# Banded attention's front: keys first, then queries, two score units, and the value tiles after them

## The reference, cut to what matters

```python
qkv = h @ w_qkv + b_qkv                       # 512 x 1536: 1024 query, 256 key, 256 value columns
q = qkv[..., :Hq * Dh]
k = qkv[..., Hq * Dh:(Hq + Hk) * Dh]
v = qkv[..., (Hq + Hk) * Dh:]
...                                           # each block of 128 queries sees its own and the previous 128 keys
s = jnp.einsum('bnqkgd,bnjkd->bnkgqj', qb, kb) * (Dh ** -0.5)
s = s - slopes * dist; s = jnp.where(mask, s, -inf)
m = jnp.maximum(s.max(axis=-1), sink)
p = jnp.exp(s - m[..., None]); denom = p.sum(axis=-1) + jnp.exp(sink - m)
o = jnp.einsum('bnkgqj,bnjkd->bnqkgd', p / denom[..., None], vb)
return o @ w_o + b_o
```

## Time and profile before

| what | value |
|---|---|
| median of 3 runs | 3056.63 us |
| profiled execution | 3055.59 us, span 3053.8 us |
| TensorE matmul busy | 2915.0 us (95%) |
| TensorE weight load busy | 2183.6 us (72%) |
| VectorE busy | 1656.4 us (54%) |
| ScalarE busy | 713.2 us (23%) |
| granted TensorE clock, mean | 0.991 of full speed |
| chain that ended last | PE 86%, DVE 6%, DMA 3%, ACT 2% |

### The profile page before, as it was taken

How to read it: one execution, slowest core, us unless ns; L and a number is a source line. 1 busy time by engine, 2 the same in 40 slices (tenths; PEclk the granted TensorE clock), 3 DMA queues, 4 the chain that set the end, 5 groups by cost and what they waited for, 6 DMA issues and landing times.

```text
span 3053.8 us, 36072 instructions
## 1 busy us (share of the span) xinstructions
PE 2915.0 (95%) x14366; PEld 2183.6 (72%) x14366; DVE 1656.4 (54%) x2731; ACT 713.2 (23%) x1346; POOL 71.7 (2%) x136
## 2 busy tenths in 40 slices
PE   7999999999899999979999989999999998999998
PEld 5888888778557888834444434478888846888887
DVE  3777777356666677640111047565555468655545
ACT  3444444220573001110000022420000016200001
POOL 0000000000000101000000001000000020000000
PEclk9999999999999999989999999999999999999999
DMA  5110010112102546369999986112222270122221
GB/s 234 61 43 35 35 70 28 63 62 83 63 15 90 198 179 216 116 261 421 422 422 422 422 336 287 58 55 79 88 83 83 111 272 33 56 83 84 102 91 55
DMA packets 71751, 451.73 MB, mean 148 GB/s; under 512 B 8032, under 2 KB 10224, under 8 KB 24112
## 3 DMA queue, kind: packets, MB, share of 16 engines
q1 hardware_dynamic: 53840, 374.17, 30.6%
q0 software_dynamic: 17040, 73.18, 6.7%
q10 hardware_dynamic: 720, 2.29, 0.2%
HBM read 445.41 MB, written 2.10 MB: 147 GB/s over the span
## 4 chain that ended last, share of the span: by engine, by line
PE 86%; DVE 6%; DMA 3%; ACT 2%; DVEq 2%; issue 1%; ACTq 0%; SPq 0%
PE PS L253 79%; DMA ring<-stream 2%; PE PS L1638 1%; PE PS L1523 1%; DVE arena L1588 1%; PE PS L1621 1%; DVE stat L1647 1%; DMA hT<-stream 1%; DMA arena<-x 1%; DVE arena L1153 1%; PE PS L2374 1%; PE PS L2354 1%; DVE PS L2705 0%; ACT arena L1541 0%; DVEq L1098 0%
## 5 line engine op out<-in xcount | busy, mean ns | idle before, releaser
L253 PE MATMUL PS<-arena 128*128 128x256 f32 (+3 forms) x4960 | 984.9, 388 | 18.6 <-ACT arena L874 8.8
L253 PEld LDWEIGHTS PS<-arena 128*128 128x128 f32 (+1 forms) x4960 | 744.8, 183 | 237.9 <-issue 151.0
L253 PE MATMUL PS<-arena,ring 128*128 128x256 f32 (+1 forms) x1992 | 467.1, 390 | 0.0
L253 PEld LDWEIGHTS PS<-arena,ring 128*128 128x128 f32 x1992 | 377.6, 190 | 74.1 <-issue 25.4
L253 PE MATMUL PS<-hT,ring 128*128 128x256 f32 (+1 forms) x1504 | 405.2, 424 | 10.6 <-ACT hT L420 6.2
L253 PEld LDWEIGHTS PS<-hT,ring 128*128 128x128 f32 x1504 | 288.4, 193 | 118.1 <-issue 80.6
L253 PE MATMUL PS<-xT,arena 128*128 128x256 f32 x1056 | 232.2, 379 | 0.0
L253 PEld LDWEIGHTS PS<-xT,arena 128*128 128x128 f32 x1056 | 200.6, 190 | 28.5 <-issue 1.4
L2128 DVE TENSOR_TENSOR arena<-arena,PS 128x512 f32<-128x512 f32 x16 | 11.0, 687 | 369.9 <-PE PS L253 369.9
L253 PE MATMUL PS<-hT,arena 128*128 128x256 f32 (+1 forms) x864 | 195.1, 442 | 1.3 <-DMA hT<-stream 1.3
L598 DVE CUSTOM_DVE_ANT_0 arena<-arena,PS 128x1024 f32<-128x1024 f32 x128 | 152.1, 1216 | 48.3 <-DMA arena<-adat 46.9
(11 more groups left out here) (310 smaller groups left out, 2999.5 us busy)
## 6 DMA issues: line engine op xcount, KB each, us to landing
ring<-stream SPq DMA_DIRECT2D x217, 1024.0 KB, 7.1
arena<-stream SPq DMA_DIRECT2D x98, 1024.0 KB, 18.7
arena<-adat POOLq DMA_DIRECT2D x88, 512.0 KB, 5.0
hT<-stream SPq DMA_DIRECT2D x32, 1024.0 KB, 18.6
arena<-adat POOLq DMA_DIRECT2D x20, 1024.0 KB, 10.1
arena<-stream SPq DMA_DIRECT2D x8, 512.0 KB, 4.4
arena<-x ACTq DMA_DIRECT2D x4, 512.0 KB, 15.4
xT<-stream SPq DMA_DIRECT2D x2, 1024.0 KB, 21.0
```

The lines of the kernel that those rows point to most:

```text
L253: ins = nc.tensor.matmul(out_, lhsT, rhs, start=start, stop=stop_, **kw)
```

## The change

The weight stream is laid out anew so that the key columns come first, then the query columns, then the value columns. TensorE computes the 2 key tiles, then the 8 query tiles, waits for a new semaphore `k_ok` and for the tenth tile's copy, and enters the attention: scores of units 0 and 1, then the two value tiles (passed in as `fill`) on banks 6 and 7, then the attention's loop. ScalarE copies the value tiles out behind the exponentials of unit 1. VectorE does 8 modulation steps, waits for the two key tiles, makes the doubled key layout, and does the other 24 steps. What followed stays in its order and ends in `k_ok`; the value bias is added in the hook behind unit 0 and raises `v_ok`, which TensorE awaits before the first values. Of the waits for weights only those at the first tile of each unit pair remain.

```diff
-        def gemm_tok(pe, g, gp, su, tok, toks, c0, ncol, kt=KT, cols=512):
+        def gemm_tok(pe, g, gp, su, tok, toks, c0, ncol, kt=KT, cols=512, bank0=0):
-            bank = gp % 2
+            bank = bank0 + gp % 2
...
-            def pe_(pe):
+            def pe_(pe, fill=None):
...
                 scores(0)
                 scores(1)
+                if fill is not None:
+                    fill(pe)
                 for u in range(n):
...
-            def act_(act):
+            def act_(act, fill=None):
...
                     if u + 1 < n:
                         exps(u + 1)
+                    if u == 0 and fill is not None:
+                        fill(act)
...
+        TILES = (8, 9, 0, 1, 2, 3, 4, 5, 6, 7)
+
         def swa_qkv_pe(pe):
             pe.wait_ge(n_r, NR[8] + 2)
             mod_sum(pe, 3)
-            for j in range(12):
-                g, su = G_SQKV + j, U_SQKV + 2 * min(j // 4, 2)
-                if j < 10:
-                    gemm(pe, g, g, su, 0, ((j % 4) * P,), hT, ready=NM[8] if j == 0 else None)
-                else:
-                    t0 = (j - 10) * 2 * P
-                    gemm_tok(pe, g, g, su, hT, (t0, t0 + P), 256, 256)
-                if j in (3, 7, 11):
+            for i in range(10):
+                g = G_SQKV + i
+                gemm(pe, g, g, U_SQKV + 2 * (i // 4), 0, ((i % 4) * P,), hT, waits=i % 4 == 0,
+                     ready=NM[8] if i == 0 else None)
+                if i in (3, 7):
                     pend[0] += 2
+
+        def swa_values_pe(pe):
+            for i in range(2):
+                g = G_SQKV + 10 + i
+                t0 = i * 2 * P
+                gemm_tok(pe, g, g, U_SQKV + 4, hT, (t0, t0 + P), 256, 256, bank0=6)
+            pend[0] += 2
             flush(pe)
 
+        def swa_values_act(act):
+            for i in range(2):
+                g = G_SQKV + 10 + i
+                evac(act, g, g, VK2[:, 2 * i:2 * i + 2, :], w=256, bank0=6)
...
-            mod_steps(v, 3, 0, 32)
-            mod_end(v, 3, ((6, 80, V_GMLP + 8),))
-            v.wait_ge(evac_done, G_SQKV + 10)
+            mod_steps(v, 3, 0, 8)
+            v.wait_ge(evac_done, G_SQKV + 2)
             for g in range(4):
                 r0 = (g % 2) * 64
                 for e in range(2):
                     nc.vector.tensor_copy(KP2[64 * e:64 * e + 64, g, :], kl2[r0:r0 + 64, g // 2, :])
+            mod_steps(v, 3, 8, 24)
+            mod_end(v, 3, ((6, 80, V_GMLP + 8),))
             nc.vector.tensor_tensor(st8[:, 0:KT], mod2[:, 64:64 + KT], V[:, V_BO:V_BO + KT], ALU.mult)
             v.drain()
             for j in range(KT):
                 nc.vector.tensor_scalar(xT[:, j, :], xT[:, j, :], st8[:, j:j + 1], None, ALU.add)
             v.wait_ge(in_pool, POOL_SWA)
             nc.vector.tensor_scalar(snk[:, 1, :], snk[:, 0, :], -1.0, None, ALU.mult)
-            v.wait_ge(evac_done, G_SQKV + 12)
-            nc.vector.tensor_tensor(VK2[:, :, :], VK2[:, :, :], bvs.unsqueeze(1).broadcast_to([P, NT, 256]),
-                                    ALU.add)
-            v.drain().then_inc(v_ok, 1)
+            v.drain().then_inc(k_ok, 1)
+
+        def swa_values_dve(v, u):
+
+            if u == 0:
+                v.wait_ge(evac_done, G_SQKV + 12)
+                nc.vector.tensor_tensor(VK2[:, :, :], VK2[:, :, :], bvs.unsqueeze(1).broadcast_to([P, NT, 256]),
+                                        ALU.add).then_inc(v_ok, 1)
...
             swa_qkv_pe(pe)
-            pe.wait_ge(v_ok, 1)
-            swa_att_pe(pe)
+            pe.wait_ge(k_ok, 1)
+            pe.wait_ge(evac_done, G_SQKV + 10)
+            swa_att_pe(pe, swa_values_pe)
...
-            parts += _chunks(a["swa_w_qkv_2"][0]) + _chunks(a["swa_w_o_2"][0])
+            qkv = a["swa_w_qkv_2"][0]
+            parts += _chunks(cat([qkv[:, D:D + 256], qkv[:, :D], qkv[:, D + 256:]], 1)) + _chunks(a["swa_w_o_2"][0])
```

More of the change, by code:

```diff
@@ L303, in gemm_tok, with evac @@
                        w[:, k % kpu, c0:c0 + ncol], k == 0, k == kt - 1, mm_done if last else None)
-        def evac(act, g, gp, dst, n=T, func=ACT.Copy, w=None, **kw):
+        def evac(act, g, gp, dst, n=T, func=ACT.Copy, w=None, bank0=0, **kw):
             act.wait_ge(mm_done, g + 1)
-            src = PS[:, gp % 2, 0:n]
+            src = PS[:, bank0 + gp % 2, 0:n]
             if w is not None:
@@ L2611, in build @@
         kl2 = area(22016, 2, T)
-        v_ok = sem("v_ok")
+        k_ok, v_ok = sem("k_ok"), sem("v_ok")
+        TILES = (8, 9, 0, 1, 2, 3, 4, 5, 6, 7)
         def swa_qkv_pe(pe):
@@ L2616, in swa_qkv_pe @@
             mod_sum(pe, 3)
-            for j in range(12):
-                g, su = G_SQKV + j, U_SQKV + 2 * min(j // 4, 2)
-                if j < 10:
-                    gemm(pe, g, g, su, 0, ((j % 4) * P,), hT, ready=NM[8] if j == 0 else None)
-                else:
-                    t0 = (j - 10) * 2 * P
-                    gemm_tok(pe, g, g, su, hT, (t0, t0 + P), 256, 256)
-                if j in (3, 7, 11):
-                    pend[0] += 2
+            for i in range(10):
[3 more added lines that the diff above has]
+                if i in (3, 7):
+                    pend[0] += 2
+        def swa_values_pe(pe):
[4 more added lines that the diff above has]
+            pend[0] += 2
             flush(pe)
+        def swa_values_act(act):
+            for i in range(2):
+                g = G_SQKV + 10 + i
+                evac(act, g, g, VK2[:, 2 * i:2 * i + 2, :], w=256, bank0=6)
         def swa_qkv_act(act):
[L2629 to L2635, removed]
+            for i, j in enumerate(TILES):
+                g = G_SQKV + i
+                dst = qn[:, j, :] if j < 8 else kl2[:, j - 8, :]
+                evac(act, g, g, dst, func=ACT.Identity, bias=V[:, V_BQKV + j:V_BQKV + j + 1])
         def swa_qkv_dve(v):
@@ L2691, in swa_value @@
             k0, nk = swa_keys(qb)
+            if u == 0:
+                pe.wait_ge(v_ok, 1)
             for k in range(2):
@@ L2715, in build @@
             lambda u, h, S: (Pb3[:, u % 2, h, 0:swa_keys(u % NT)[1] * P], four(S, swa_keys(u % NT)[1] * P)[:, h, :]),
-            lambda u, h: Pb3[:, u % 2, h, 0:swa_keys(u % NT)[1] * P], swa_maximum, 0.125, sink=True)
+            lambda u, h: Pb3[:, u % 2, h, 0:swa_keys(u % NT)[1] * P], swa_maximum, 0.125, sink=True, beside=swa_values_dve)
         xf = area(0, KT, T)
@@ L2858, in _ @@
             swa_qkv_act(act)
-            swa_att_act(act)
+            swa_att_act(act, swa_values_act)
             residual_act(act, N_SWO, 9)
```

## The result

The changed kernel takes 3064.2 us, the median of 22 runs (3058.19 to 3069.6); the kernel before, run beside it, 3056.64 (22 runs, 3054.85 to 3064.24). The ratio is 1.0022, 95% interval 1.0016 to 1.0028, or some 6.7 us slower; the two medians lie 7.6 us apart. The profiled execution has a span of 3061.8 us against 3053.8.

What follows compares the result with a forecast made beforehand. TensorE, never idle, was taken to bound the projections and VectorE the attention. Third peak 5.48 late, plus 1.23 value bias, minus 0.45 recovered, made 6.26, say +6.3: 3061.9 profiled, 3062.9 median; range 3058.8 to 3066.0 us.

Steps and rivals of the forecast that it cites:

- The pause set by `k_ok`: Between tenth tile and first scores: TensorE stands 8.3 us, from 2520.92 to 2529.20, waiting for VectorE's chain.
- The copies among the steps: VectorE's key copies behind the eighth modulation step shift a load and delay the last step by 2.0 us, bounds 0 and 3.45.
- GpSimd's load under the copies: By the skill's port rule, the load at 2471.70 starts its bytes only behind the copies, delay nearer the upper bound, 3.45.
- The clock behind the pause: After TensorE's pause ahead of the scores, its clock falls to half, costing 2.4 us, bounds 1.7 and 3.2.
- Scores of unit 2: Behind the value tiles, TensorE needs 0.76 us of these scores before the third peak may start.
- Value bias: On VectorE between peak 2 and division 1 in the attention: costs 1.23 us, bounds 0 and 1.5.
- What comes back: VectorE's wait for the fifth peak's scores goes, as TensorE runs at full clock: 0.45 us recovered, bounds 0 and 0.8.
- The remaining units are as before: From the fifth peak's recovered wait on, VectorE's chain over the attention's remaining units is unchanged, adding nothing.
- a change of VectorE's pace: Sign of being wrong: VectorE's pace in the attention changes; no size given.
- A: Rival: key copies don't delay the modulation steps and the clock costs 1.7; +3.6 us, 3060.2; chance 0.18.
- B: Rival: nothing is made up, the last modulation step is delayed 3.45, clock costs 3.2; +8.5 us, 3065.2; chance 0.15.
- C: Rival: modulation steps end early at 2517.8, pause 1.0 us, clock holds; -3.4 us, 3053.2; chance 0.05 including full overlap.

Runs made afterwards that it cites:

- e3: Changed kernel with the 8 key copies put back behind all 32 modulation steps: 3064.34 us, ratio 1.0024 to the kernel before.
- e4: Changed kernel with six unused 128x512 matmuls added in TensorE's pause ahead of the first scores: 3061.55 us, ratio 1.0012 to the kernel before.
- e5: Changed kernel with the value bias done in two halves ahead of the third peak: 3061.32 us, ratio 1.0016 to the kernel before.
- e1: The changed kernel run and profiled again, nothing altered: 3062.49 us, ratio 1.0019 to the kernel before.
- e6: Changed kernel with the value tiles ahead of the scores again: 3057.65 us, ratio 1.0002 to the kernel before.
- e8: Changed kernel with the modulation's row in banks 4 and 5 and k_ok raised behind the key copies: 3056.7 us, ratio 1.0003 to the kernel before.
- e7: As e8, plus modulation's end, output bias and halved value bias ahead of the third peak: 3051.98 us, ratio 0.9987 to the kernel before.
- e2: Changed kernel with the output bias taken out of k_ok's wait, done behind unit 0's division: 3058.86 us, ratio 1.0005 to the kernel before.

## Why the prediction was right

The forecast was slower by 6.3 us, 3062.9; measured 3064.2, ratio 1.0022. The mechanism of the front held: a pause set by `k_ok`, half the clock behind it, and the value bias in VectorE's chain. That the stretch came out at 6.21 is luck in part: up to the fifth peak the terms add up to 4.78 and not 6.26, and 1.4 us that the prediction didn't have came behind it. And the runs of the changed kernel alone spread over 11 us, so that its median lies 1.3 from the forecast says less than the terms do.

- **The pause set by `k_ok`.** Right in kind. Predicted 8.3 us, measured 6.08 and 6.23. The chain behind the last step with the hand-over was nearly as summed: 4.12 us predicted (0.45 + 3.59 + 0.08), 4.41 measured (2524.41 to 2528.82). (The slack of VectorE's chain before the change is 4.14 us, 2530.59 to 2534.73, not 4.2.)
- **The copies among the steps.** This is the mis-sized term. I put the delay of the last step at 2.0; it was none (e3: 1.71 without the copies among the steps, 1.66 and 1.82 with them). DMA time was lost as I had reasoned: from 2478 to 2480 the share was 0.40 at 82 GB/s (before, 0.98 at 377). But the steps behind the copies ran without any wait, four in a row from 2476.38, and VectorE's waits for these loads fell from 24.5 to 20.6 us. What it lost was made up in later waits. The last three waits for loads were 3.36, 2.55 and 0.86 us before and 3.33, 2.55 and 1.36 after; ahead of them, SyncE had issued two 1 MB loads of the stream (after, at 2509.9 and 2510.3). That these set the end of the steps is likely, but not shown.

The window of the changed kernel just behind the copies (columns as above):

```profile
2478.00:2480.00 2.00, 2.00 (x6) 0.90 (x5) 2.00 (x5) 0.00 (x0) 0.96 (x2) 1.00 0.40 82
```

- **GpSimd's load under the copies.** The load at 2473.28 lay under them; GpSimd spent 0.59 us on it instead of 0.53, and it landed after 5.8 us, where the three loads ahead of it took 4.9, 4.9 and 5.8. The 0.59 came again in all seven other profiles with the copies there. The load's bytes did not wait for the copies to end: by the packet records of e4 and e5 its first packet went 0.8 and 0.6 us before that, right behind the load ahead of it. The Trainium skill (SBUF — State Buffer, section "SBUF: two separate sides") has descriptors held up while such a copy runs; the prediction took eight copies of 0.43 us for one. Held up for all eight they were not, and the measurement decides.
- **The clock behind the pause.** Predicted 2.4, measured 2.3 to 2.4 at the third peak and 2.5 to 2.6 from the first scores (e4); the longer scores and value tiles add up to 1.35 + 1.32 = 2.7 against the kernel before. Right.
- **Scores of unit 2.** Predicted 0.76, from the row of unit 0; measured 1.18 (2547.09 to 2548.27). Unit 0 has 128 keys, unit 2 has 256: I read the duration from the wrong shape. The third peak was then 4.17 late (25.52 less 21.35) where 5.48 was predicted. In the profile's own times it came at 2548.27, 6.0 behind 2542.27, which looks like the 5 to 6 of the prediction, but 1.83 of it was there ahead of the change.
- **Value bias.** Predicted 1.23, measured 1.13 (e5).
- **What comes back.** Predicted 0.45; from peak 4 to peak 5 it took 3.57 instead of 4.10, so 0.53. At the fifth peak the changed kernel was 4.78 late, 1.5 less than forecast.
- **"The remaining units are as before".** That sentence failed, and brought the sum back to 6.2; a change of VectorE's pace was one of the prediction's own signs of being wrong. The clock fell inside the attention in every profile of a kernel with the changed order but e5. In the first profile 1.4 us were added behind the fifth peak (6.21 less 4.78): 0.3 of it by the seventh, at full clock, and 1.2 behind that, where the clock was at half at 76.0 (41.45 us from peak 7 to the output projection; 40.30 in e1, whose clock did not fall there, and 40.29 before). In e1 2.5 us were added (7.35 less 4.86), all of it by the seventh peak. The kernel before has such a fall too, at 21.7. I had priced the clock where TensorE comes out of a pause, and not where it is fed in small pieces by VectorE.
- **Rivals.** A (the copies are free) was right on its first half; its price of the clock, 1.7, was too low (2.5), and its +3.6 missed the second fall. B and C did not come. That the loss is the wait for `k_ok` ahead of the scores is shown from two sides: by e6, which gives TensorE other work for that time, and by e8, which takes the wait away.

What stays open: why the clock falls in the attention in one execution and not in the next. The changed kernel's runs lie between 3058 and 3070 us, e7's between 3051 and 3057; profiles show falls at other places, but no run here held their cause apart. One thing fits: with the value bias between peak and division, TensorE stands 3.2 us ahead of unit 1's transposes (after, e1 to e4, e8), with the bias ahead of the peak 2.10 (e5, e7). e5 had no fall in the attention and e7 a short one, while e1, e2, e3 and e8 had one of 6.8 us there; but e4 had a short one, and after none until its end. It would also say why e7's median is 4.7 us below e8's, where the bias alone is 1.1. That is argued, not shown.

## What to carry to other kernels

Work that is brought forward on one engine is bounded by what that engine then waits for: look first for the semaphore, and for the shared bank or buffer that forces it so late. Here the modulation's row in banks that the scores overwrite put 24 steps ahead of it, and a residual update that the scores don't need stood there too. With TensorE free of both (e8) the same order of work takes the time of before and not 7 us more; with the biases also moved ahead of the third peak (e7) it is 4 us faster. And work hidden beside a long dense block loses its cover when that block is moved behind it.

## What the runs showed of the hardware

- Six matmuls with no use, 5.31 us in a pause of 6.3, kept the granted clock at 1.0 and made the value tiles 1.2 us shorter (14.08 for 15.30, e4).
- A granted clock of 0.50 for 6.8 us cost 2.2 us inside a stage that VectorE bounds (e1, peak 4 to 7), though TensorE had pauses there: transposes, values and scores in a row (1.97, 1.98 and 1.59 us) became longer than VectorE's unit, which then waited 2.47 us.
- A DMA share of 0.91 to 0.95 over 13 to 16 us did not mean that a gap in the issue of loads delays the last of them: with the 3.46 us of copies among the steps the last step ended 1.66 and 1.82 us behind the tenth tile, without them 1.71 (e3).
- A GpSimd issue of a 512 KB load under eight VectorE copies of 64x512 took 0.59 us and not 0.53. In e4 the load's first packet went at 2472.36, with the copies running until 2473.19.
